# Two mixers' value projections in panels of 4 x 128 input features by 512 output features, summed over two panels in one bank

## What is computed

```python
def mixer_a(h, w_in, v_gain, w_s, b_s, w_out):
    bsz, S, _ = h.shape
    proj = h @ w_in
    u = proj[..., :A_WIDTH]
    v = rms_norm(proj[..., A_WIDTH:2 * A_WIDTH], v_gain)
    z = proj[..., 2 * A_WIDTH:]
    nc = S // CHUNK
    v = v.reshape(bsz, nc, CHUNK, A_GROUPS, A_GROUP_DIM)
    ...
    mixed = jnp.einsum('gij,bcjgd->bcigd', ws, v) + b_s.T[None, None, :, :, None]
    mixed = mixed.reshape(bsz, S, A_WIDTH)
    y = u * mixed * jax.nn.silu(z)
    return y @ w_out
```

## Time and profile before

| | us |
|---|---|
| median of 3 runs | 3306.97 |
| lowest and highest of them | 3304.75, 3308.42 |
| the profiled execution | 3309.21 |
| its span in the profile | 3307.5 |
| mean granted TensorE clock, share of full | 0.983 |

### The profile page before, as it was taken

How to read it: one execution, slowest core, us unless ns; L and a number is a source line. 1 busy time by engine, 2 the same in 40 slices (tenths; PEclk the granted TensorE clock), 3 DMA queues, 4 the chain that set the end, 5 groups by cost and what they waited for, 6 DMA issues and landing times.

```text
span 3307.5 us, 39150 instructions
## 1 busy us (share of the span) xinstructions
PE 3184.5 (96%) x16114; PEld 2628.3 (79%) x16114; DVE 1640.6 (50%) x2141; ACT 1100.9 (33%) x1448; POOL 1558.2 (47%) x1138
## 2 busy tenths in 40 slices
PE   6999999999999999999999999989999999989998
PEld 5988878787878788789887877766888877768887
DVE  5763565657574443534636666665212266542223
ACT  3222233434343332232212434444222343242222
POOL 3544466556463454444443511126445565344444
PEclk9999999999999999999999999999999999989999
DMA  4544421122121232245444211112332332122331
GB/s 144 178 166 140 140 100 64 65 67 73 64 76 52 89 102 90 89 128 179 166 140 149 64 51 35 35 40 79 108 98 93 102 128 89 64 64 90 101 100 66
DMA packets 279315, 320.03 MB, mean 97 GB/s; under 512 B 6866, under 2 KB 245089, under 8 KB 278946
## 3 DMA queue, kind: packets, MB, share of 16 engines
q1 hardware_dynamic: 240960, 247.48, 23.3%
q10 hardware_dynamic: 38178, 70.06, 6.3%
HBM read 311.22 MB, written 6.29 MB: 96 GB/s over the span
## 4 chain that ended last, share of the span: by engine, by line
PE 87%; DVE 6%; ACT 3%; POOL 2%; issue 1%; DMA 1%; ACTq 0%; SPq 0%; DVEq 0%; POOLq 0%
PE ps L536 24%; PE ps L538 23%; PE ps L537 23%; PE psx L961 2%; POOL Wl L344 1%; PE psx L733 1%; PE ps L993 1%; PE ps L777 1%; PE psx L711 1%; ACT Wh L1209 1%; PE psx L536 1%; PE psx L537 1%; PE psx L538 1%; PE psx L750 1%; PE psx L627 1%
## 5 line engine op out<-in xcount | busy, mean ns | idle before, releaser
L344 POOL TENSOR_TENSOR Wl<-Wr,Wh 128x512 fp32r<-128x512 f32 x928 | 1276.7, 1407 | 1527.4 <-ACT Wh L1209 1523.2
L536 PE MATMUL ps<-Ah,Wh 128*128 128x512 f32 x1920 | 773.6, 403 | 6.5 <-POOL Wl L344 6.5
L538 PE MATMUL ps<-Ah,Wl 128*128 128x512 f32 x1920 | 749.8, 390 | 0.0
L537 PE MATMUL ps<-Al,Wh 128*128 128x512 f32 x1920 | 749.4, 390 | 0.0
L1209 ACT ACTIVATE Wh<-Wr 128x2048 fp32r<-128x2048 f32 x232 | 442.9, 1909 | 368.2 <-DMA Wr<-in_w_mlp_in_dram 111.4
L536 PEld LDWEIGHTS ps<-Ah,Wh 128*128 128x128 f32 x1920 | 361.5, 188 | 92.4 <-issue 11.1
L536 PE MATMUL ps<-Yh,Wh 128*128 128x512 f32 x1088 | 426.4, 392 | 4.4 <-issue 2.7
L537 PEld LDWEIGHTS ps<-Al,Wh 128*128 128x128 f32 x1920 | 361.6, 188 | 83.5 <-issue 10.3
L537 PE MATMUL ps<-Yl,Wh 128*128 128x512 f32 x1088 | 424.6, 390 | 0.0
L538 PE MATMUL ps<-Yh,Wl 128*128 128x512 f32 x1088 | 424.5, 390 | 0.0
L538 PEld LDWEIGHTS ps<-Ah,Wl 128*128 128x128 f32 x1920 | 361.1, 188 | 76.4
(11 more groups left out here) (401 smaller groups left out, 4111.1 us busy)
## 6 DMA issues: line engine op xcount, KB each, us to landing
Wr<-in_a_w_in_dram SPq DMA_DIRECT2D x48, 1024.0 KB, 6.6
modw<-in_w_mod_dram ACTq DMA_DIRECT2D x96, 512.0 KB, 5.5
Wr<-in_b_w_in_dram SPq DMA_DIRECT2D x40, 1024.0 KB, 5.0
Wr<-in_w_mlp_in_dram SPq DMA_DIRECT2D x32, 1024.0 KB, 5.7
Wr<-in_w_mlp_out_dram SPq DMA_DIRECT2D x32, 1024.0 KB, 5.1
Wr<-in_a_w_out_dram SPq DMA_DIRECT2D x16, 1024.0 KB, 5.2
Wr<-in_c_w_in_dram SPq DMA_DIRECT2D x16, 1024.0 KB, 5.7
Wr<-in_attn_w_qkv_dram SPq DMA_DIRECT2D x12, 1024.0 KB, 5.1
```

Source lines behind the costliest of these rows:

```text
L344: last = pool.tensor_tensor(E.Wl[:, s, part], E.Wr[:, s, part], E.Wh[:, s, part].bitcast(F32), ALU.subtract)
L536: pe.matmul(o, ah, bh, start=first, stop=False)
L537: pe.matmul(o, ah, bl, start=False, stop=False)
L538: return pe.matmul(o, al, bh, start=False, stop=last)
```

## The change

The eight panels of a values phase get another shape: 4 x 128 input features by 512 output features, also one megabyte. Panel (m, h) has the input half h of the output columns 512m to 512m + 511. `wide_t` takes the place of `first_t` and `tile_t` there. Bank t belongs to token block t, for each m. In the half h = 0 it starts the sum of all four banks with 12 matmuls of 512 columns each, and h = 1 goes on with each and ends it, bank by bank. At the begin of h = 0 it waits for all four banks to be emptied. ScalarE squares and VectorE copies a full bank of 512 columns at a time. The modulation steps keep their count, and follow the banks: one behind each bank, where each m has four; those of m = 0 stand two behind bank 1 and one behind banks 2 and 3. `mod_sum` follows the first tile of m = 1, 2, 3. The columns of the z, u and output panels stay as they were.

```diff
--- before.py
+++ after.py
@@ -124,14 +124,15 @@
 
     src, at = [], {}
 
-    def add(w, k0, n0, *name):
+    def add(w, k0, n0, *name, kt=KD):
         at[name] = len(src)
-        src.append(w.rearrange("(k p) n -> p k n", p=P)[:, k0:k0 + KD, n0:n0 + 256])
+        src.append(w.rearrange("(k p) n -> p k n", p=P)[:, k0:k0 + kt, n0:n0 + 2048 // kt])
 
     def mixer_a(L, j):
         win, wout = I["a_w_in"][j], I["a_w_out"][j]
-        for n in range(8):
-            add(win, 0, AW + n * 256, L, "v", n)
+        for m in range(4):
+            for h in range(2):
+                add(win, 4 * h, AW + m * 512, L, "v", m, h, kt=4)
         for half in range(2):
             for q in range(4 * half, 4 * half + 4):
                 add(win, 0, 2 * AW + q * 256, L, "z", q)
@@ -261,11 +262,6 @@
-def v_bank(n, u):
-
-    return 2 * u if n == 0 else 2 * ((n + 1) % 2) + u
@@ -363,8 +359,9 @@
         pool.wait_ge(*E.signals["ld_a"].of(L, "bs"))
         pool.affine_select(out=E.wsr, in_=E.wsr, compare_op=ALU.is_ge, fill=0.0, base=0,
                            pattern=[[0, 8], [-1, P]], channel_multiplier=1).then_inc(*G.did("cm", L))
-        for n in range(8):
-            ahead(L, "v", n)
+        for m in range(4):
+            for h in range(2):
+                ahead(L, "v", m, h)
         for half in range(2):
             for q in range(4 * half, 4 * half + 4):
                 ahead(L, "z", q)
@@ -579,22 +576,38 @@
                     m.then_inc(*T.did(*events[f]))
                     emptied[b] = emptied_by[f]
 
-    def first_t(L, p):
+    def wide_t(L, p, m, h, between):
+
+
+        def triple(t, k, ops):
+            for W, lhs, start, stop in ops:
+                i = pe.matmul(bank[t], lhs[:, 4 * h + k, t * P:(t + 1) * P], part(W, p, k, 0, 512, 4), start=start, stop=stop)
+            return i
 
         for t in range(TT):
-            into(t)
-        for k in range(KD):
-            pe.wait_ge(*A.of("nh", L, k))
+            if h == 0:
+                into(t)
+        if m + h == 0:
+            for k in range(4):
+                pe.wait_ge(*A.of("nh", L, k))
+                for t in range(TT):
+                    triple(t, k, [(E.Wh, Ah, k == 0, False), (E.Wl, Ah, False, False)])
+                pe.wait_ge(*h_ready(L)(k))
+                for t in range(TT):
+                    i = triple(t, k, [(E.Wh, Al, False, False)])
+        else:
             for t in range(TT):
-                for W in (E.Wh, E.Wl):
-                    pe.matmul(bank[t][:, 0:256], Ah[:, k, t * P:(t + 1) * P], part(W, p, k, 0, 256, KD), start=(k == 0 and W is E.Wh), stop=False)
-            pe.wait_ge(*h_ready(L)(k))
-            for t in range(TT):
-                m = pe.matmul(bank[t][:, 0:256], Al[:, k, t * P:(t + 1) * P], part(E.Wh, p, k, 0, 256, KD), start=False, stop=(k == KD - 1))
-                if k == KD - 1 and t % 2:
-                    m.then_inc(*T.did(L, "v", 0, t // 2))
-        for t in range(TT):
-            emptied[t] = V.of(L, "v", 0, t // 2)
+                for k in range(4):
+                    if m == 0 and t == 0:
+                        pe.wait_ge(*h_ready(L)(4 + k))
+                    i = triple(t, k, [(E.Wh, Ah, h + k == 0, False), (E.Wl, Ah, False, False), (E.Wh, Al, False, h == 1 and k == 3)])
+                if h:
+                    i.then_inc(*T.did(L, "v", m, t))
+                    emptied[t] = V.of(L, "v", m, t)
+                if m and h + t == 0:
+                    between(m)
+        if h == 0:
+            i.then_inc(*T.did(L, "vk", m))
 
     def h_ready(L):
         return lambda k: (G if k % 2 else V).of("h", L, k)
@@ -678,16 +691,11 @@
                     m = pe.matmul(psx[:, 1, c:c + 1], t[:, r * P:(r + 1) * P], ones[:, 0:1], start=True, stop=True)
                 m.then_inc(*X.did("modsum", L, nb, who))
 
-        for n in range(8):
-            p = begin(L, "v", n)
-            if n == 0:
-                first_t(L, p)
-            else:
-                for u in range(2):
-                    tile_t(p, (2 * u, 2 * u + 1), Ah, Al, v_bank(n, u), (L, "v", n, u), V.of(L, "v", n, u))
-                    if n % 2 + u == 0:
-                        mod_sum(n // 2 - 1)
-            used(p)
+        for m_ in range(4):
+            for h in range(2):
+                p = begin(L, "v", m_, h)
+                wide_t(L, p, m_, h, lambda m: mod_sum(m - 1))
+                used(p)
         pe.wait_ge(*G.of("cm", L))
         for g in range(8):
             b = 2 + g // 4
@@ -1318,29 +1326,28 @@
                 act.wait_ge(*V.of("modr", L, *((nb, kp - 2) if kp >= 2 else (nb - 1, kp + 2))))
             act.dma_start(E.modw[:, kp % 2, :, :], src).then_inc(*MODW[kp % 2].did(L, nb, kp))
 
-        for n in range(8):
-            q = n % 2
-            if n < 2:
-                mod_load(0, 2 * n)
-            if n == 0:
-                mod_load(0, 1)
-            for u in range(2):
-                b = v_bank(n, u)
-                act.wait_ge(*T.of(L, "v", n, u))
-                if n >= 2:
-                    act.wait_ge(*V.of("ss", L, n - 2))
-                for jj in range(2):
-                    t = 2 * u + jj
-                    if n + u:
-                        act.wait_ge(*A.of(L, "vq", n if u else n - 1, (2 * u + jj - 2) % 4))
-                    act.activation(sq[:, jj, 0:256], ps[b][:, jj * 256:(jj + 1) * 256] if n else ps[b + jj][:, 0:256], ACT.Square,
-                                   accum_out=ssA[:, 4 + 4 * q + t:5 + 4 * q + t]).then_inc(*A.did(L, "vq", n, t))
+        for m in range(4):
+            ahead(L, "v", m, 0)
+            for t in range(TT):
+                n, u = 2 * m + t // 2, t % 2
+                if u == 0 and n < 2:
+                    mod_load(0, 2 * n)
+                if n + u == 0:
+                    mod_load(0, 1)
+                act.wait_ge(*T.of(L, "v", m, t))
+                if m >= 2:
+                    act.wait_ge(*V.of("ss", L, m - 2))
+                if m or t >= 2:
+                    act.wait_ge(*A.of(L, "vq", *((m, t - 2) if t >= 2 else (m - 1, t + 2))))
+                c = 4 + 4 * (m % 2) + t
+                act.activation(sq[:, t % 2, :], ps[t][:], ACT.Square, accum_out=ssA[:, c:c + 1]).then_inc(*A.did(L, "vq", m, t))
                 if n and u == 0:
-                    mod_load(n // 2, 2 * q + 1)
+                    mod_load(n // 2, 2 * (n % 2) + 1)
                 elif 0 < n < 7:
-                    mod_load((n + 1) // 2, 2 * (1 - q))
-            ahead(L, "v", n)
-        act.wait_ge(*V.of("ss", L, 7))
+                    mod_load((n + 1) // 2, 2 * (1 - n % 2))
+                if t == 1:
+                    ahead(L, "v", m, 1)
+        act.wait_ge(*V.of("ss", L, 3))
         act.activation(ssA[:, 12:16], ssA[:, 0:4], ACT.Sqrt, bias=eps[:, 0:1], scale=1.0 / AW).then_inc(*A.did(L, "vrms"))
         for half in range(2):
             for q in range(4 * half, 4 * half + 4):
@@ -1903,20 +1910,18 @@
                         V.also("mac", L, nb, who)
             V.also("modr", L, nb, kp)
 
-        for n in range(8):
-            q = n % 2
-            for u in range(2):
-                b = v_bank(n, u)
-                dve.wait_ge(*T.of(L, "v", n, u))
-                dve.wait_ge(*A.of(L, "vq", n, 2 * u + 1))
-                for jj in range(2):
-                    dve.tensor_scalar(vA[:, 2 * u + jj, n * 256:(n + 1) * 256], ps[b][:, jj * 256:(jj + 1) * 256] if n else ps[b + jj][:, 0:256], 1.0, None,
-                                      ALU.mult).then_inc(*V.did(L, "v", n, u))
-                if u:
-                    dve.wait_ge(*(V.of("ss", L, n - 1) if n else V.of("ss0", L)))
-                    dve.tensor_tensor(ssA[:, 0:4], ssA[:, 0:4], ssA[:, 4 + 4 * q:8 + 4 * q], ALU.add).then_inc(*V.did("ss", L, n))
+        for m in range(4):
+            for t in range(TT):
+                n, u = 2 * m + t // 2, t % 2
+                dve.wait_ge(*T.of(L, "v", m, t))
+                dve.wait_ge(*A.of(L, "vq", m, t))
+                dve.tensor_scalar(vA[:, t, m * 512:(m + 1) * 512], ps[t][:], 1.0, None, ALU.mult).then_inc(*V.did(L, "v", m, t))
+                if t == 3:
+                    dve.wait_ge(*(V.of("ss", L, m - 1) if m else V.of("ss0", L)))
+                    c = 4 + 4 * (m % 2)
+                    dve.tensor_tensor(ssA[:, 0:4], ssA[:, 0:4], ssA[:, c:c + 4], ALU.add).then_inc(*V.did("ss", L, m))
                 if n:
-                    mod_use(n // 2, 2 * q + u)
+                    mod_use(n // 2, 2 * (n % 2) + u)
                 elif u:
                     mod_use(0, 0)
                     mod_use(0, 1)
```

## The result

The changed kernel takes 3342.02 us (median of 4 runs, 3340.69 to 3344.54) against 3307.69 for the kernel before (median of 4; the table ahead has three of them): ratio 1.0102, 95% interval 1.0086 to 1.0118. It is slower by 34.3 us where +40 was forecast (3347, range 3322 to 3364). Its profiled execution has a span of 3341.3 us.

What follows compares the result with a forecast made beforehand. TensorE, busy 96% of the span, was taken as the bound. The terms -13.7 + 23.9 + 11.9 + 3.5 + 14.4 gave +40.0 us, so 3347 us against the median of 3306.97, range 3322 to 3364.

Steps and rivals of the forecast that it cites:

- wide matmuls and first panel, both mixers: Values phases: 10.4 us saved by wider matmuls and 3.3 us by the first panel's end, 13.7 us together.
- idle at A0's boundaries: TensorE waits for bank 3's emptying at A0's three boundaries: 9.1 + 7.4 + 7.4 = 23.9 us added.
- idle at A3's boundaries: TensorE waits for bank 3's emptying at A3's three boundaries: 4.9, 3.5 and 3.5 us, 11.9 us added.
- the clock: TensorE falls to half clock after all six boundaries, losing 2.4 us each: 14.4 us added.
- end of A0's phase: z's first tile waits 1.2 us for bank 2, the last modulation sums 2.3 us for step 3: 3.5 us added.
- The width: Values matmuls: one 512-column step takes 0.2265 us against 0.2400 for two of 256, saving 13.5 ns a pair.
- rival (d): Values matmuls: a wide one takes 0.240 us or the page's small difference holds, 8 to 10 us more, 3356; chance 0.05.
- The schedule: VectorE at boundaries: three modulation steps stand ahead of bank 3's copy, so TensorE waits 3.5 to 9.1 us each.
- The split: VectorE multiplications beside GpSimd's split step by 1.70 us instead of 0.67; clean, the waits would be 14.6 and 6.4 us.
- (a): Boundaries: multiplications and split don't meet, 21.0 us of waits, the clock falls at four: +17 us, 3324; chance 0.14.
- (b): Modulation blocks land later, 5.9 us instead of 4.9: 14 us on top of the forecast, 3361; chance 0.07.
- (c): VectorE keeps up, steps within 2.0 us, each boundary costs 1.6 us, no clock fall: -3.9 us, 3303; chance 0.06.

Runs made afterwards that it cites:

- kernel 2: Changed kernel with each bank waited for at its own tile and the modulation sums behind the fourth tile of the first half: 3297.7 us, ratio 0.9972.
- kernel 5: kernel 2 with each 512-column values matmul cut into two of 256 columns: 3309.2 us, ratio 1.0009.
- kernel 8: Changed kernel without the second (context's) modulation vector in A0, so a step is two multiplications and it computes something else: 3328.37 us, ratio 1.0061.
- kernel 3: Changed kernel with ScalarE rounding panel 2m+3 behind bank 3's square instead of bank 1's, so GpSimd's split comes later: 3330.74 us, ratio 1.0069.
- kernel 7: Changed kernel with unused filler matmuls ahead of the bank waits, 36, 26, 26 in A0 and 18, 10, 10 in A3: 3331.59 us, ratio 1.0078.
- kernel 6: kernel 2 and kernel 3 together, against the kernel before: 3302.19 us, ratio 0.9988.
- kernel 1: Changed kernel with each bank waited for ahead of its own first matmul in m = 1, 2, 3: 3350.13 us, ratio 1.0128.
- kernel 4: Changed kernel with unused filler matmuls ahead of the bank waits, 24 per boundary in A0 and 8 in A3: 3334.48 us, ratio 1.0077.

## Why the prediction was right, step by step

| term of the sum | predicted us | measured us | from |
|---|---|---|---|
| wide matmuls and first panel, both mixers | -13.7 | -13.8 | kernel 2's phases, 102.2 - 95.4 and 98.6 - 91.6 |
| idle at A0's boundaries | +23.9 | +21.6 | waits after |
| idle at A3's boundaries | +11.9 | +10.6 | waits after |
| the clock | +14.4 | +15.0 | what is left of the phases: 33.4 + 13.8 - 21.6 - 10.6 |
| end of A0's phase | +3.5 | +2.4 | 1.5 + 0.9 |
| sum | +40.0 | +35.8 | the times: +34.3 |

The mechanism and the direction were right, and each term came near its forecast. The clock's 15.0 is a remainder, not a measurement of its own. The profiled spans differ by 33.8 us; the 2.0 us to 35.8 lie outside the phases (0.5 ahead of A0, 0.9 between A0 and A3, 0.6 behind A3).

- **The width.** The step of 0.2265 us, taken from matmuls of the other orientation, held: 0.227. By the figures of the Trainium skill (TensorE: Matmul & The Clock Gate, "Back-to-back issue gap"), which that section gives for a single matmul by itself, the width would have been worth an estimated 1.0 us a mixer; A3's phases of kernels 2 and 5 differ by 4.7. The trace was the better source, and rival (d) falls.
- **The schedule.** It put the boundaries at 9.1, 7.4, 7.4, 4.9, 3.5 and 3.5 us; they are 8.9, 6.2, 6.4, 4.8, 2.9 and 2.9. The mechanism, three steps ahead of bank 3's copy, is shown by kernels 2 and 8. The six waits together were off by a tenth, the shorter boundaries by a sixth. The largest misses, at A0's second and third boundary, did not come from the split: bank 0 was full at 92.35, and the split ran from 98.44 to 104.76, so 6.1 to 12.4 us behind it, as forecast. VectorE was ahead of the schedule instead. Step 0 has two cheap first operations (0.40 us each instead of 0.67), so it takes 2.1 us instead of 2.7. The blocks landed in 3.7 us instead of the 4.9 used, so step 1 began at 4.2 and 4.4 instead of 4.95 and had three of its four multiplications done clean instead of two. Half a us was in the working itself: a step 2 that starts at 10.35, is stretched until 12.4 and then clean ends at 14.3, not 14.8. (The same arithmetic puts the two steps of m = 0 at 13.4, not 13.1.) At A0's first boundary and at A3's three the split did begin 0.7 us early, 5.3 us behind bank 0, and ended within half a us of the forecast. The panels landed in 5.9 us in A0 instead of 6.8:

```profile
modw<-in_w_mod_dram ACTq DMA_DIRECT2D x13, 512.0 KB, 3.7
Wr<-in_a_w_in_dram SPq DMA_DIRECT2D x6, 1024.0 KB, 5.9
```

  Why both land sooner than in the earlier trace rows was not tried. The panels' rows are now two kilobytes long instead of one, and the loads meet at other times.
- **The split.** Kernel 3 took 10.8 us of bank waits off A0 and 4.0 off A3, so counting the multiplications as stretched was right; clean ones would have forecast 14.6 us in A0 and 6.4 in A3, and the kernel without the overlap has 10.8 and 6.6.
- **The clock.** 2.4 us a boundary: kernel 7 says 2.1 by its time and 2.3 by its phases, the account 2.5. That the clock would fall at all six was argued from their length being over 3.27 us; two of them turned out at 2.89, and it fell there too, so this part was in some measure luck. Kernel 3 shows that length alone doesn't decide.
- **Rivals.** (a) is what kernel 3 builds, 3330.7 where 3324 was said, and the changed kernel is not it. (b) didn't occur; the loads were earlier, not later. (c) fell: A0's steps took 2.1, 3.7 and 5.1 us at its second boundary, where 2.0 was the limit.
- **What the prediction didn't see:** that two places in TensorE's order (where the banks are waited for and where the sums stand), and not the change's shape, made the loss. It priced the wait for all banks at once and never asked what a wait for each would cost.

## What to carry to other kernels

Price a wider matmul by the distance of starts in a full stream, not by the mean duration of its group: here 13.5 ns for a pair, not 173. When a change bundles what arrived evenly into bursts, write down the other engine's order between two bursts, and ask what stands ahead of the last buffer; its average load doesn't show it (VectorE is busy for 65.9 of 95.4 us in A0's phase of kernel 2, which has hardly a wait). Then look for the two waits that can be moved behind the burst: with each bank waited for at its own tile and the sums behind the fourth one, the same change gives 3297.7 instead of 3342.0 us, 0.28% faster than the kernel before (interval 0.16 to 0.39%).

## What the runs showed of the hardware

- The clock can fall when TensorE is back at work. Behind the second boundary of A3 (2.89 us idle) the first matmul lasts 0.47 us, at full clock, and only from 1.2 us later on do they last 0.59 and then 0.63:

```profile
1529.34 0.47 PE L584 MATMUL ps<-Wh,Ah 128*128 128x512 f32 x1 [2.89 <-DVE vA L1918]
...
1530.95 0.63 PE L584 MATMUL ps<-Wh,Ah 128*128 128x512 f32 x1
```

- The length of an idle time alone does not say whether the clock falls: in kernel 3, 2.72 us were followed by half clock and 2.73 us were not (experiment 3).
- One-column matmuls did not keep the clock up. An idle time of 1.64 us with them behind it was followed by half clock (kernel 7, A3), one of 1.67 with wide matmuls behind it was not (kernel 3, twice in A3); kernel 7 had 0.78 us of idle time some 4 us earlier too, so the two places differ in more than this. In kernel 6 half clock came with 2.1 us of idle time and some 2 us of sums. Filler matmuls of 512 columns into a bank that nobody reads did keep it up (kernel 7), and took 10.4 us off.
- The same untouched code behind A3 took 1757 to 1761 us in most profiled executions and 1766 to 1767 in those of kernels 1, 4 and 8, with a lower granted clock in the attention. A difference of 6 us between two executions can come from there, and some of kernel 8's 13.7 and kernel 4's 7.5 us can be hidden by it.
